# One turn of eight experts: the largest expert's overflow moves into four column strips and shares its turn with the smallest expert

## The chip, the cores and the metric

The kernel runs on one core of a Trainium2 chip. The metric is the time of one execution in microseconds (us). A core has TensorE (PE in the profile, its weight loads are PEld), VectorE (DVE), ScalarE (ACT), GpSimd (POOL) and SyncE (SP), which here issues the DMAs.

## The reference

Two layers over 256 latent tokens and 256 context tokens of width 1024. The last sub-layer of the second layer is a mixture of eight SwiGLU experts, two for each token. Only that part is touched by the change.

```python
N_EXPERTS = 8; TOP_K = 2; D_EXPERT = 3584; D_MODEL = 1024

def moe_swiglu(h, router_w, w1, w3, w2):
    logits = (h @ router_w).astype(jnp.float32)
    top_v, top_i = lax.top_k(logits, TOP_K)
    top_p = jax.nn.softmax(top_v, axis=-1)
    comb = jnp.sum(jax.nn.one_hot(top_i, N_EXPERTS, dtype=jnp.float32) * top_p[..., None], axis=-2).astype(h.dtype)
    y = jnp.zeros_like(h)
    for e in range(N_EXPERTS):
        y = y + comb[..., e:e + 1] * swiglu(h, w1[e], w3[e], w2[e])
    return y
```

Every tensor is float32. With the inputs that the reference draws (seed 0) its router sends 78, 61, 147, 94, 22, 46, 21 and 43 tokens to experts 0 to 7, worked out with the reference itself.

## The kernel before

**Experts, columns, turns.** Each expert gets only the tokens that chose it, gathered into slots. Expert 0 is column 0. The other seven are sorted by their token count on the chip: column 1 is the largest, column 2 the next, column 7 the third of them, and columns 3 to 6 the rest in falling order. `CAPS` gives the slots of each column. An expert with more tokens than slots gets its remaining tokens in an additional pass of a hardware loop at the end, `n_loop` of which always runs once for the last column.

The work is laid out in turns (`KINDS`, then one loop pass of kind S):

- **M**: one expert in 128 slots. Each weight unit is split by ACT (`w_hi`, L1355) and DVE (`w_lo`, L1713) into a high and a low part, and each product is three matmuls (`three`, L577 to L579) with 512 moving columns.
- **S**: one expert in 64 slots, no split. The weight unit in float32 is the moving operand, the 64 slots are the stationary operand in one half of the array's columns; the two halves (column strips of 64) work on different columns of the weights. Up part L1198, down part L1247.
- **P**: an M expert and an S expert at a time, each with its own weights.
- **B**: the largest expert alone, its first 128 slots as in M and 64 more as in S, from the same weight units.

Before, the turns are M, S, P, S, B, S and the loop pass S: seven turns for eight experts. `turn_m` and `turn_s` transpose the hidden values, `spread_of` turns a one-hot matrix, `scatter` puts the outputs back into token order in banks 6 and 7, and DVE adds them into an accumulator.

**Units and their ring.** An expert is 84 units of 512 KB: 56 for the up and gate matrices (7 column blocks `cb` of 8 units) and 28 for the down matrix. Units are loaded by SP in the order of `UNITS`. In P it is four units of the M expert, then four of the S expert, and so on. They land in a ring of 14 slots (`M_RING`). `moe_free` holds SP at L529 until the slot's former unit is done with: for kind "m" that is when DVE has split it (`lo_done`), for "s" and "b" when TensorE has used it (`s_used`). The split parts live in a second ring of 6 (`R`), and DVE and ACT split up to 5 units ahead (`LEAD`).

**Order on TensorE in a turn with both.** For each half `w` of each block: the M products of 4 units (24 matmuls), then the strips of 4 units, then, once a block, the transposes of the block before. In the down part: M products of 4 units, then the strips of 4 units. `gather_m` (L1051) and `gather_s` (L1062) collect the next turn's tokens in the third block of the down part. A matmul in float32 with both operands float32 (the strips) leaves two records in the trace, one with the split operands leaves one.

Of the kernel before, what the change touches and what calls it, by code (L numbers as in the profile page):

```python
# [152 lines left out]
def steps_of(kind):  # L153

    return {"M": [("m", 0), ("m", 1)], "S": [("s", 0), ("s", 1)],
            "B": [("m", 0), ("m", 1), ("s", 0), ("s", 1)], "P": [("m", 0), ("m", 1), ("s", 0), ("s", 1)]}[kind]
# [25 lines left out]
S_AT = {(tau, v): n for n, (tau, part, v) in enumerate(UNITS) if part != "m"}  # L182
# [40 lines left out]
def build(nc, x, c, ctx_in, c_ctx, w_ada, b_ada, norm_mix, norm_ffn, norm_out, w_in_even, gmlp_wt, gmlp_b,  # L223
# [3 lines left out]
    with es:  # L227
# [41 lines left out]
        cw_s = sb("cw_s", [P, LT])  # L269
        cslot_s = sb("cslot_s", [P, 1])  # L270
# [76 lines left out]
        sx_y, sx_sc, s_used = sem("sx_y"), sem("sx_sc"), sem("s_used")  # L347
        fin32, fin_tr, fin_out, stored = sem("fin32"), sem("fin_tr"), sem("fin_out"), sem("stored")
# [68 lines left out]
        def _(sp):  # L417
# [113 lines left out]
            def moe_free(n):  # L531

                if n < R:
                    u = max(u for u in range(U_MOE) if u % R == n)
                    sp.wait_ge(lo_done, u + 1)
                elif n < M_RING:
                    sp.wait_ge(h_done, 4 * KT)
                else:
                    tau, part, v = UNITS[n - M_RING]
                    if part == "m":  # L540
                        sp.wait_ge(lo_done, U_MOE + m_index(tau) * EXP_UNITS + v + 1)
                    else:
                        sp.wait_ge(s_used, s_index(tau) * EXP_UNITS + v + 1)
# [30 lines left out]
        def _(pe):  # L574
# [548 lines left out]

            def moe_turn(kind, tau, m, s, prev, adds, nxt):

                has_m, has_s, both = kind != "S", kind != "M", kind in ("B", "P")
# [8 lines left out]
                def old_outputs(v):  # L1135

                    if v in places:
                        x = places.index(v)
                        what, half = steps[x]
                        scatter(what, prev_m if what == "m" else prev_s, half, adds if x < 2 else adds + 1,  # L1140
                                prev_s if prev_kind in ("B", "P") and x == 0 else None)
# [17 lines left out]
                if has_m:  # L1159

                    pe.wait_ge(ga_lo, m + 1)
                if has_s:

                    pe.wait_ge(sx_g, tally(s, 1, 1))
                for cb in range(CB):
# [5 lines left out]
                    for w in range(2):  # L1171
# [19 lines left out]
                        if has_s:  # L1191
# [24 lines left out]
                    if cb == 3 and both:  # L1216

                        pe.wait_ge(sp_rdy, m + 1)
                        spread_of(onehot_s, cw_s).then_inc(sx_sp, 1)

                if prev_kind in ("M", "B", "P"):

                    pe.wait_ge(ey32, prev_m + 1)
                if prev_kind in ("S", "B", "P"):
# [7 lines left out]
                for cb in range(CB):  # L1232
# [9 lines left out]
                    if has_s:  # L1242
                        pe.wait_ge(sx_t, tally(s, CB, cb + 1))
                        for kt in range(4 * cb, 4 * cb + 4):
# [11 lines left out]
                    if cb == 2:  # L1256
# [3 lines left out]
                        if next_kind != "M":  # L1260
                            gather_s(next_s, 5 if next_kind in ("B", "P") else 0)
# [78 lines left out]
        def _(act):  # L1340
# [294 lines left out]
            def turned_s(s, cb, bank):  # L1635

                act.wait_ge(sx_mm, tally(s, CB, cb + 1))
                dst = hidden_s[:, cb * 4 * HALF:(cb + 1) * 4 * HALF].rearrange("p (j q c) -> p q j c", j=2, q=2)
                act.activation(dst, ps[:, bank, 0:256].rearrange("p (q j c) -> p q j c", q=2, j=2),
                               ACT.Copy).then_inc(sx_t, 1)  # L1640

            def moe_turn(kind, tau, m, s, prev, nxt):

                has_m, has_s, both = kind != "S", kind != "M", kind in ("B", "P")
                prev_kind, prev_m, prev_s = prev
                for v in range(EXP_UNITS):
                    if isinstance(tau, int):
                        split_to(min(splits_by(tau, v), U_MOE + len(M_ORDER)))
                    if v == 1 and prev_kind in ("M", "B", "P"):
                        out_hi(prev_m)  # L1650
                    if v % 8 == 0 and 8 <= v <= UP_UNITS:
# [5 lines left out]
                        if has_s:  # L1657
                            act.wait_ge(s_used, tally(s, EXP_UNITS, v))
                            gate = ps[:, 3 if both else 2 * (cb % 2), 0:256]
                            act.activation(ar(X_SS, 256), gate, ACT.Silu).then_inc(sx_silu, 1)  # L1660
                    if v % 8 == 4 and 12 <= v <= UP_UNITS + 4:
# [3 lines left out]
                        if has_s:  # L1665
                            turned_s(s, cb, (5, 3)[cb == CB - 1] if both else 6)
                    if v == UP_UNITS + 12:
# [3 lines left out]
                        if next_kind != "M":  # L1671
                            gathered_s(next_s, 5 if next_kind in ("B", "P") else 0)
# [26 lines left out]
        def _(dve):  # L1699
# [471 lines left out]
            def route_levels():  # L2171
# [5 lines left out]
                link(dve.memset(cap[:, 1:2], float(SLOTS + HALF)))  # L2177
# [49 lines left out]
            def one_hots_s(col, first):  # L2227
# [8 lines left out]
                dve.tensor_copy(cw_s[:, :].unsqueeze(2), src).then_inc(sx_oh, 1)  # L2236
# [12 lines left out]
            def out_scale_s(s, bank):  # L2249

                dve.wait_ge(s_used, tally(s, EXP_UNITS, EXP_UNITS))
                dve.wait_ge(sx_spr, tally(s, 1, 1))
                dve.tensor_scalar(ar(X_YS, BANK), ps[:, bank, :], cslot_s[:, 0:1], None, ALU.mult).then_inc(sx_y, 1)
# [22 lines left out]
            def moe_turn(kind, tau, m, s, prev, adds, nxt, m_col, s_col):  # L2276

                has_m, has_s, both = kind != "S", kind != "M", kind in ("B", "P")
# [3 lines left out]
                for v in range(EXP_UNITS):  # L2282
                    if isinstance(tau, int):
                        split_to(min(splits_by(tau, v), U_MOE + len(M_ORDER)))
                    if v == 0 and prev_kind in ("M", "B", "P"):
                        out_scale(prev_m)
                    if v == 0 and prev_kind in ("S", "B", "P"):
                        out_scale_s(prev_s, 4 if prev_kind == "S" else 7)
                    if v in (1, 2) and prev_kind in ("M", "B", "P"):
# [5 lines left out]
                    if v % 8 == 0 and 8 <= v <= UP_UNITS:  # L2295
# [5 lines left out]
                        if has_s:  # L2301
# [4 lines left out]
                            up = ps[:, 3, 256:512] if both else ps[:, 2 * (cb % 2) + 1, 0:256]  # L2306
                            dve.tensor_tensor(ar(X_HS, 256), up, ar(X_SS, 256), ALU.mult).then_inc(sx_hid, 1)  # L2307
# [6 lines left out]
                    if v == (33 if both else 25) and has_s:  # L2314
                        dve.wait_ge(sx_sp, tally(s, 1, 1))
                        dve.tensor_copy(ar(X_SPR, N_LAT), ps[:, 7, 0:256])
                        dve.tensor_copy(cslot_s[:, :], ps[:, 7, 256:257]).then_inc(sx_spr, 1)
# [10 lines left out]
                    if v == UP_UNITS + 5:  # L2328
                        if nxt != "S":
                            one_hots(m_col)  # L2330
                        if nxt != "M":
                            one_hots_s(s_col, SLOTS if nxt == "B" else 0)
# [64 lines left out]
```

## Time and profile before

| | |
|---|---|
| median of 3 runs | 2117.19 us (2114.79 to 2118.25) |
| the profiled execution | 2117.6 us, its span 2115.8 us |
| granted TensorE clock, mean | 0.945 |
| TensorE busy | 1896.9 us (90%) |
| VectorE, ScalarE busy | 916.8 us (43%), 729.6 us (34%) |
| DMA | 479.54 MB, mean 227 GB/s |

The table is of the profile's page. Shares of the whole span are a mean over stages that have different limits, so the rows to read are those of one turn at a time: how long it lasts, how busy TensorE is in it, and what the DMA engines move. A busy TensorE is not yet a full one, since ends of matmuls are modelled and overlap; the starts of successive groups are the better measure.

### The profile page before, as it was taken

To read this page: it belongs to the slowest core of one execution; us is meant where nothing else is said; L and a number is where in the kernel's file an instruction comes from. 1 tells how busy PE (TensorE), PEld (TensorE's weight loads), DVE (VectorE), ACT (ScalarE), POOL (GpSimd) and SP (SyncE) were. 2 spreads that over 40 slices of the span, in tenths; PEclk is the share of its full clock that TensorE was granted. 3 is DMA by queue.
4 is the path that set the end of the run, shared out by engine and by line. 5 is a ranking of instruction groups with operands and counts; after the bars stand their busy time and mean duration, and the time that the engine had idled before them with its cause. 6 is when DMAs were issued, how large, how long until landed. Compare 5 with 4: busy or idle time off the path is not lost.

```text
span 2115.8 us, 25988 instructions
## 1 busy us (share of the span) xinstructions
PE 1896.9 (90%) x10266; PEld 1346.8 (64%) x10266; DVE 916.8 (43%) x1290; ACT 729.6 (34%) x938; POOL 114.1 (5%) x122
## 2 busy tenths in 40 slices
PE   5999899999997788796659999999999999999987
PEld 2677577777785677676657874566654577664433
DVE  2432622332235656867647940355530366530002
ACT  3231221221223645555436730244420345410001
POOL 0000000000000122423300000000000000000000
PEclk8998999999998899898868999999999999999998
DMA  8634166343431322210136989999999965579994
GB/s 320 230 129 139 30 239 235 115 138 130 149 100 40 100 61 69 60 60 21 60 129 228 375 327 409 409 409 408 409 409 409 380 219 213 202 296 408 409 409 185
DMA packets 161692, 479.54 MB, mean 227 GB/s; under 512 B 14961, under 2 KB 58145, under 8 KB 155426
## 3 DMA queue, kind: packets, MB, share of 16 engines
q1 hardware_dynamic: 161570, 477.88, 60.4%
q8 instruction: 81, 1.33, 0.3%
q14 instruction: 41, 0.34, 0.0%
HBM read 476.77 MB, written 1.05 MB: 226 GB/s over the span
## 4 chain that ended last, share of the span: by engine, by line
PE 65%; DVE 12%; DMA 11%; SPq 4%; ACT 4%; issue 3%; POOL 1%; DVEq 0%; ACTq 0%
PE ps L577 13%; PE ps L579 13%; PE ps L578 13%; PE ps L1198 9%; PE ps L1247 4%; DMA arena<-in_moe_up 4%; SPq L529 4%; DMA arena<-in_moe_w 4%; DMA raw<-in_moe_up 3%; DVE w_lo L1713 3%; PE ps L591 2%; PE ps L610 2%; PE ps L1062 1%; ACT w_hi L1355 1%; DVE arena L1770 1%
## 5 line engine op out<-in xcount | busy, mean ns | idle before, releaser
L1713 DVE TENSOR_TENSOR w_lo<-raw,w_hi 128x1024 fp32r<-128x1024 f32 x242 | 302.7, 1258 | 455.2 <-ACT w_hi L1355 450.7
L1355 ACT ACTIVATE w_hi<-raw 128x1024 fp32r<-128x1024 f32 x242 | 254.0, 1056 | 463.3 <-PE ps L579 383.4
L577 PE MATMUL ps<-h_hi,w_hi 128*128 128x512 f32 (+1 forms) x736 | 292.8, 398 | 26.2 <-DVE h_lo L1757 22.8
L578 PE MATMUL ps<-h_hi,w_lo 128*128 128x512 f32 (+1 forms) x736 | 283.0, 385 | 0.0
L579 PE MATMUL ps<-h_lo,w_hi 128*128 128x512 f32 (+1 forms) x736 | 282.3, 384 | 0.0
L1713 DVE TENSOR_TENSOR w_lo<-arena,w_hi 128x1024 fp32r<-128x1024 f32 x144 | 173.6, 1222 | 91.7 <-ACT w_hi L1355 85.6
L577 PEld LDWEIGHTS ps<-h_hi,w_hi 128*128 128x128 f32 x736 | 147.5, 200 | 83.2 <-issue 53.7
L1198 PE MATMUL ps<-arena 128*64 128x256 f32 x1536 | 188.0, 385 | 13.3 <-DMA arena<-in_moe_up 7.1
L1355 ACT ACTIVATE w_hi<-arena 128x1024 fp32r<-128x1024 f32 x144 | 152.0, 1060 | 116.7 <-PE ps L579 46.8
L579 PEld LDWEIGHTS ps<-h_lo,w_hi 128*128 128x128 f32 x736 | 146.2, 199 | 26.2
L578 PEld LDWEIGHTS ps<-h_hi,w_lo 128*128 128x128 f32 x736 | 147.2, 200 | 23.8 <-issue 0.5
L1198 PEld LDWEIGHTS ps<-arena 128*64 128x64 f32 x1536 | 102.2, 136 | 87.9 <-DMA arena<-in_moe_up 28.0
L1198 PE MATMUL ps<-raw,arena 128*64 128x256 f32 x1152 | 137.8, 384 | 7.7 <-DMA raw<-in_moe_up 4.5
L577 PE MATMUL ps<-w_hi,s_hi 128*128 128x512 f32 x336 | 135.9, 404 | 4.3 <-DVE s_lo L2217 2.4
L579 PE MATMUL ps<-w_lo,s_hi 128*128 128x512 f32 x336 | 132.2, 393 | 0.0
L578 PE MATMUL ps<-w_hi,s_lo 128*128 128x512 f32 x336 | 132.1, 393 | 0.0
L577 PE MATMUL ps<-w_hi,h_hi 128*128 128x512 f32 (+1 forms) x328 | 118.2, 360 | 6.3 <-DVE arena L1914 6.3
L1198 PEld LDWEIGHTS ps<-raw,arena 128*64 128x64 f32 x1152 | 78.1, 137 | 62.6 <-DMA raw<-in_moe_up 18.8
L578 PE MATMUL ps<-w_hi,h_lo 128*128 128x512 f32 (+1 forms) x328 | 115.3, 351 | 0.0
L579 PE MATMUL ps<-w_lo,h_hi 128*128 128x512 f32 (+1 forms) x328 | 115.1, 351 | 0.0
L1247 PE MATMUL ps<-arena,scratch 128*64 128x512 f32 x384 | 97.4, 623 | 7.6 <-DMA arena<-in_moe_w 6.9
L2307 DVE TENSOR_TENSOR arena<-ps,arena 128x256 f32<-128x256 f32 x42 | 17.7, 422 | 194.8 <-ACT arena L1660 194.8
(345 smaller groups left out, 2507.7 us busy)
## 6 DMA issues: line engine op xcount, KB each, us to landing
arena<-in_moe_up SPq DMA_DIRECT2D x256, 512.0 KB, 9.9
raw<-in_moe_up SPq DMA_DIRECT2D x192, 512.0 KB, 9.4
arena<-in_moe_w SPq DMA_DIRECT2D x128, 512.0 KB, 12.8
raw<-in_moe_w SPq DMA_DIRECT2D x96, 512.0 KB, 14.2
raw<-in_ffn_w SPq DMA_DIRECT2D x66, 512.0 KB, 5.4
arena<-in_w_ada SPq DMA_DIRECT2D x32, 1024.0 KB, 5.4
raw<-in_w_in_odd SPq DMA_DIRECT2D x40, 512.0 KB, 3.5
scratch<-in_w_ada SPq DMA_DIRECT2D x16, 1024.0 KB, 5.7
```

Source lines behind the costliest of these rows:

```text
L529: sp.dma_start(moe_slot(n), src).then_inc(moe_in[n % M_RING], 16)
L577: pe.matmul(dst, s_h, m_h, start=start, stop=False, **kw)
L578: pe.matmul(dst, s_l, m_h, start=False, stop=False, **kw)
L579: return pe.matmul(dst, s_h, m_l, start=False, stop=stop, **kw)
L591: m = pe.matmul(ps[32 * j:32 * j + 32, bank, :], cond[:, a % KT, :], w[:, j * BANK:(j + 1) * BANK], start=start, stop=stop, skip_group_che ...
L610: pe.matmul(ps[:, 3, 0:width], ones, ar(NORM_AT[n] + kt % 2 * NT, width), start=(kt == 0), stop=(kt == KT - 1)).then_inc(sq_mm, 1)
L1062: i = pe.matmul(ps[:, bank, kt * HALF:(kt + 1) * HALF], part[:, t * D + kt * P:t * D + (kt + 1) * P], onehot_s[:, t, 0:HALF], start=(q == ...
L1198: i = pe.matmul(ps[64 * j:64 * j + 64, bank, at:at + 256], ar(X_G + kt * HALF, HALF), src[:, kk * BANK + 256 * j:kk * BANK + 256 * j + 256 ...
L1247: i = pe.matmul(ps[64 * j:64 * j + 64, 7 if both else 4, :], hidden_s[:, kt * HALF:(kt + 1) * HALF], src[:, j * BANK:(j + 1) * BANK], star ...
L1355: act.activation(w_hi[:, o % R, :], src, ACT.Copy).then_inc(hi_done, 1)
L1713: dve.tensor_tensor(w_lo[:, o % R, :], src, w_hi[:, o % R, :].bitcast(F32), ALU.subtract).then_inc(lo_done, 1)
L1770: m = dve.tensor_scalar(t[:, a:b], t[:, a:b], coef[:, kt, s:s + 1], adaT[:, layer, sh * KT + kt, s:s + 1], ALU.mult, ALU.add)
```

## The change

The turns become M, Q, S, P, S and the loop pass S: six turns for the same eight experts. The new kind Q runs column 1 (the largest) in 128 slots as in M with 32 more slots, and column 6 (the smallest) in 32 slots. Both groups of 32 slots are computed in column strips of 32, four at a time: strip `j` takes a quarter of the moving columns, 128 in the up part and 256 in the down part. The group `q = 0` reads the largest expert's units again (kind "b"), the group `q = 1` the smallest one's (kind "s"). A slot with a "b" unit comes free when `q = 0` has used it (`qx_used`). The caps become 128, 160, 128, 64, 64, 64, 32, 64. The largest expert's turn is now the second, right behind M, and kind B is gone. All units of all experts are loaded once, as before.

```diff
-KINDS = "MSPSBS"
-M_COL = {0: 0, 2: 2, 4: 1}
-S_COL = {1: 3, 2: 4, 3: 5, 4: 1, 5: 6, 6: 7}
-CAPS = [SLOTS, SLOTS + HALF, SLOTS, HALF, HALF, HALF, HALF, HALF]
+QUART = SLOTS // 4
+KINDS = "MQSPS"
+M_COL = {0: 0, 1: 1, 3: 2}
+S_COL = {1: 6, 2: 3, 3: 4, 4: 5, 5: 7}
+Q_TURN = KINDS.index("Q")
+S_BANK = {"S": 0, "P": 5, "Q": 7}
+CAPS = [SLOTS, SLOTS + QUART, SLOTS, HALF, HALF, HALF, QUART, HALF]
...
-            for part in {"M": "m", "S": "s", "B": "b", "P": "ms"}[kind]:
+            for part in {"M": "m", "S": "s", "Q": "bs", "P": "ms"}[kind]:
...
                     if part == "m":
                         sp.wait_ge(lo_done, U_MOE + m_index(tau) * EXP_UNITS + v + 1)
+                    elif part == "b":
+                        sp.wait_ge(qx_used, v + 1)
                     else:
...
+                if kind == "s" and n == s_index(Q_TURN):
+                    for k in range(4):
+                        dst = ps[:, 6 + k // 2, k % 2 * 256:k % 2 * 256 + 256]
+                        j = (4 * half + k) // 2 * QUART
+                        for q in range(2):
+                            at = X_YS + q * 256 + k % 2 * P
+                            i = pe.matmul(dst, arena[j:j + QUART, at:at + P],
+                                          arena[j:j + QUART, X_SPR + q * N_LAT:X_SPR + (q + 1) * N_LAT],
+                                          start=(q == 0), stop=(q == 1), tile_position=(j, 0))
+                    i.then_inc(sx_sc, 1)
+                    return
...
+            def spread_strips(q):
+
+                for t in range(LT):
+                    hot = onehot_s[:, t, q * QUART:(q + 1) * QUART].bitcast(F32)
+                    for j in range(4):
+                        pe.matmul(ps[j * QUART:(j + 1) * QUART, 7, t * P:(t + 1) * P], hot, ident, start=True, stop=True,
+                                  skip_group_check=True)
...
+                        if quart:
+                            for q in range(2):
+                                for k in range(4):
+                                    src = s_unit(v + k) if q else x_unit(v + k)
+                                    for kk in range(2):
+                                        kt = 2 * k + kk
+                                        rows = ar(X_G + kt * HALF + q * QUART, QUART)
+                                        for j in range(4):
+                                            at = 256 * q + P * w
+                                            i = pe.matmul(ps[j * QUART:(j + 1) * QUART, 3, at:at + P], rows,
+                                                          src[:, kk * BANK + P * j:kk * BANK + P * (j + 1)],
+                                                          start=(kt == 0), stop=(kt == KT - 1), skip_group_check=True)
+                                    i.then_inc(s_used if q else qx_used, 1)
+                        elif has_s:
...
+                            if both and cb == 1 and prev_kind in ("M", "Q", "P"):
+
+                                pe.wait_ge(ey32, prev_m + 1)
...
+                        if quart:
+                            spread_strips(0).then_inc(qx_sp, 1)
+                        else:
+                            spread_of(onehot_s, cw_s).then_inc(sx_sp, 1)
+                    if cb == 4 and quart:
+
+                        pe.wait_ge(qx_spr, 1)
+                        spread_strips(1).then_inc(sx_sp, 1)
...
+                    if quart:
+                        for q in range(2):
+                            for kt in range(4 * cb, 4 * cb + 4):
+                                src = s_unit(UP_UNITS + kt) if q else x_unit(UP_UNITS + kt)
+                                rows = hidden_s[:, kt * HALF + q * QUART:kt * HALF + (q + 1) * QUART]
+                                for j in range(4):
+
+                                    i = pe.matmul(ps[j * QUART:(j + 1) * QUART, 7, 256 * q:256 * q + 256], rows,
+                                                  src[:, 256 * j:256 * j + 256], start=(kt == 0 and q == 0),
+                                                  stop=(kt == EXP_KT - 1), skip_group_check=True)
+                                i.then_inc(s_used if q else qx_used, 1)
```

ACT and DVE follow with the same number of instructions in a block: the gate, the product and the turned copy address the strips' values in the new order, DVE scales the two halves of the output one by one, and copies the spread matrix in two parts (at units 33 and 41). `one_hots_q` makes the two one-hot matrices.

## Rows read from the trace of the kernel before

**Rows 1.** The page: the span in 40 slices of 52.9 us each.

```profile
PE   5999899999997788796659999999999999999987
...
PEclk8998999999998899898868999999999999999998
DMA  8634166343431322210136989999999965579994
GB/s 320 230 129 139 30 239 235 115 138 130 149 100 40 100 61 69 60 60 21 60 129 228 375 327 409 409 409 408 409 409 409 380 219 213 202 296 408 409 409 185
```

**Rows 2.** Busy time by stretches: turns S, P, S, B, the last two.

```profile
core 0: us, PE busy (x) PEld busy (x) DVE busy (x) ACT busy (x) POOL busy (x), PEclk, DMA share, GB/s
1247.60:1347.50 99.90, 95.26 (x661) 49.79 (x660) 12.96 (x24) 11.33 (x21) 0.00 (x0) 0.97 1.00 396
1347.50:1565.30 217.80, 209.53 (x1168) 144.31 (x1168) 113.76 (x114) 95.04 (x112) 0.00 (x0) 0.99 1.03 409
1565.30:1672.20 106.90, 98.14 (x679) 50.58 (x675) 13.63 (x25) 9.12 (x18) 0.00 (x0) 1.00 1.03 409
1672.20:1879.60 207.40, 207.40 (x1166) 143.31 (x1168) 117.73 (x115) 100.91 (x113) 0.00 (x0) 1.00 0.63 225
1879.60:2090.00 210.40, 192.49 (x1277) 91.32 (x1274) 18.27 (x35) 11.96 (x30) 0.00 (x0) 0.99 0.99 394
```

**Rows 3.** Waits of SP's queue inside turn B (1680 to 1895 us): total, times, longest.

```profile
SPq L529 <- PE ps L1198: 112.1, 63, 8.1
SPq L529 <- PE ps L1247: 54.5, 26, 9.8
```

**Rows 4.** Timeline of TensorE in turn B without the M products: start, length, what.

```profile
1758.96 1.95 PE L1198 MATMUL ps<-raw,arena 128*64 128x256 f32 x16
1760.73 1.90 PE L1198 MATMUL ps<-arena 128*64 128x256 f32 x16
1762.56 0.66 PE L1076 MATMUL ps<-con,arena 128*128 128x128 f32 x4
1763.05 0.38 PE L1088 MATMUL ps<-con,arena 128*128 128x128 f32 x2
1768.85 3.67 PE L1198 MATMUL ps<-arena 128*64 128x256 f32 x32
1778.12 1.95 PE L1198 MATMUL ps<-arena 128*64 128x256 f32 x16
...
1797.28 3.67 PE L1198 MATMUL ps<-arena 128*64 128x256 f32 x32
```

**Rows 5.** Timeline of TensorE, down part of turn B: its strips.

```profile
1866.87 3.65 PE L1247 MATMUL ps<-arena,scratch 128*64 128x512 f32 x16
1876.12 3.65 PE L1247 MATMUL ps<-arena,scratch 128*64 128x512 f32 x16
```

**Rows 6.** Timeline of weight loads at 30 us: strips of 32 columns, 512 moving.

```profile
30.01 0.13 PEld L591 LDWEIGHTS ps<-arena,cond 128*32 128x32 f32 x4 [0.30 <-issue]
30.44 0.13 PEld L591 LDWEIGHTS ps<-arena,cond 128*32 128x32 f32 x4 [0.30 <-issue]
30.87 0.13 PEld L591 LDWEIGHTS ps<-arena,cond 128*32 128x32 f32 x4 [0.30 <-issue]
```

**Rows 7.** Timeline of TensorE before turn B: both gathers (L1051, start of L1062).

```profile
1649.01 2.00 PE L1051 MATMUL ps<-onehot,s_hi 128*128 128x128 f32 x16
1650.85 1.95 PE L1051 MATMUL ps<-onehot,s_lo 128*128 128x128 f32 x16
1652.64 0.35 PE L1062 MATMUL ps<-onehot_s,s_hi 128*128 128x64 f32 x2
1652.83 0.39 PE L1062 MATMUL ps<-onehot_s,s_lo 128*128 128x64 f32 x2
1653.05 0.39 PE L1062 MATMUL ps<-onehot_s,s_hi 128*128 128x64 f32 x2
```

**Rows 8.** Busy time by stretches, columns as in rows 2: right behind turn M.

```profile
1248.00:1249.00 1.00, 1.00 (x14) 0.64 (x11) 0.98 (x1) 0.00 (x0) 0.00 (x0) 1.00 0.00 0
```

**Rows 9.** DMA issues in turn B: count, KB each, median us from issue to landing.

```profile
arena<-in_moe_up SPq DMA_DIRECT2D x22, 512.0 KB, 5.3
raw<-in_moe_up SPq DMA_DIRECT2D x16, 512.0 KB, 4.9
```

**Rows 10.** Waits of TensorE in turn P (1360 to 1575 us).

```profile
PE ps L1198 <- DVE arena L2307: 6.5, 6, 1.4
```

**Rows 11.** The down strips over the span: durations, first and last start.

```profile
L1247 PE MATMUL ps<-arena,scratch x384: 592/592/1116, 1315.7 to 2087.8; 128*64 128x512 f32 x192
L1247 PE MATMUL ps<-raw,scratch x288: 592/592/1061, 1308.1 to 2078.4; 128*64 128x512 f32 x144
```

**Rows 12.** The up strips over the span: count, durations, first and last start.

```profile
L1198 PE MATMUL ps<-arena x1536: 379/379/431, 1252.8 to 2050.9; 128*64 128x256 f32 x192
L1198 PE MATMUL ps<-raw,arena x1152: 379/379/431, 1247.6 to 2040.2; 128*64 128x256 f32 x192
```

More of the change, by code:

```diff
@@ L155, in steps_of @@
     return {"M": [("m", 0), ("m", 1)], "S": [("s", 0), ("s", 1)],
-            "B": [("m", 0), ("m", 1), ("s", 0), ("s", 1)], "P": [("m", 0), ("m", 1), ("s", 0), ("s", 1)]}[kind]
+            "Q": [("m", 0), ("m", 1), ("s", 0), ("s", 1)], "P": [("m", 0), ("m", 1), ("s", 0), ("s", 1)]}[kind]
 def adds_before(tau):
@@ L181 @@
 M_AT = {(tau, v): n for n, (tau, part, v) in enumerate(UNITS) if part != "s"}
-S_AT = {(tau, v): n for n, (tau, part, v) in enumerate(UNITS) if part != "m"}
+S_AT = {(tau, v): n for n, (tau, part, v) in enumerate(UNITS) if part == "s"}
 M_ORDER = [M_AT[tau, v] for tau in range(FIXED) if KINDS[tau] != "S" for v in range(EXP_UNITS)]
@@ L347, in build @@
         sx_y, sx_sc, s_used = sem("sx_y"), sem("sx_sc"), sem("s_used")
+        qx_used, qx_sp, qx_spr = sem("qx_used"), sem("qx_sp"), sem("qx_spr")
         fin32, fin_tr, fin_out, stored = sem("fin32"), sem("fin_tr"), sem("fin_out"), sem("stored")
@@ L1122, in spread_of @@
                 return i
+            def spread_strips(q):
[4 more added lines that the diff above has]
+                                  skip_group_check=True)
+                for t in range(LT):
+                    hot = onehot_s[:, t, q * QUART:(q + 1) * QUART].bitcast(F32)
+                    for j in range(4):
+                        i = pe.matmul(ps[j * QUART:(j + 1) * QUART, 7, 256:257], hot, cw_s[:, q * LT + t:q * LT + t + 1],
+                                      start=(t == 0), stop=(t == LT - 1), skip_group_check=True)
+                return i
             def moe_turn(kind, tau, m, s, prev, adds, nxt):
-                has_m, has_s, both = kind != "S", kind != "M", kind in ("B", "P")
+                has_m, has_s, both, quart = kind != "S", kind != "M", kind in ("Q", "P"), kind == "Q"
                 prev_kind, prev_m, prev_s = prev
@@ L1140, in old_outputs @@
                         scatter(what, prev_m if what == "m" else prev_s, half, adds if x < 2 else adds + 1,
-                                prev_s if prev_kind in ("B", "P") and x == 0 else None)
+                                prev_s if prev_kind in ("Q", "P") and x == 0 else None)
                 def m_unit(v):
@@ L1633, in turned_hi, with turned_s @@
                 act.activation(h_hi[:, cb * BANK:(cb + 1) * BANK], ps[:, 6, :], ACT.Copy).then_inc(et_hi, 1)
-            def turned_s(s, cb, bank):
+            def turned_s(s, cb, bank, quart):
                 act.wait_ge(sx_mm, tally(s, CB, cb + 1))
-                dst = hidden_s[:, cb * 4 * HALF:(cb + 1) * 4 * HALF].rearrange("p (j q c) -> p q j c", j=2, q=2)
-                act.activation(dst, ps[:, bank, 0:256].rearrange("p (q j c) -> p q j c", q=2, j=2),
-                               ACT.Copy).then_inc(sx_t, 1)
+                dst = hidden_s[:, cb * 4 * HALF:(cb + 1) * 4 * HALF]
+                if quart:
+                    dst = dst.rearrange("p (j q c) -> p q j c", j=4, q=2)
+                    out_of = ps[:, bank, 0:256].rearrange("p (q j c) -> p q j c", q=2, j=4)
+                else:
+                    dst = dst.rearrange("p (j q c) -> p q j c", j=2, q=2)
+                    out_of = ps[:, bank, 0:256].rearrange("p (q j c) -> p q j c", q=2, j=2)
+                act.activation(dst, out_of, ACT.Copy).then_inc(sx_t, 1)
             def moe_turn(kind, tau, m, s, prev, nxt):
-                has_m, has_s, both = kind != "S", kind != "M", kind in ("B", "P")
+                has_m, has_s, both, quart = kind != "S", kind != "M", kind in ("Q", "P"), kind == "Q"
                 prev_kind, prev_m, prev_s = prev
@@ L1648, in moe_turn @@
                         split_to(min(splits_by(tau, v), U_MOE + len(M_ORDER)))
-                    if v == 1 and prev_kind in ("M", "B", "P"):
+                    if v == 1 and prev_kind in ("M", "Q", "P"):
                         out_hi(prev_m)
@@ L1658, in moe_turn @@
                             act.wait_ge(s_used, tally(s, EXP_UNITS, v))
-                            gate = ps[:, 3 if both else 2 * (cb % 2), 0:256]
-                            act.activation(ar(X_SS, 256), gate, ACT.Silu).then_inc(sx_silu, 1)
+                            if quart:
+                                act.wait_ge(qx_used, v)
+                                gate = ps[:, 3, :].rearrange("p (q w c) -> p q w c", q=2, w=2)[:, :, 0]
+                                act.activation(ar(X_SS, 256).rearrange("p (q c) -> p q c", q=2), gate,
+                                               ACT.Silu).then_inc(sx_silu, 1)
+                            else:
+                                gate = ps[:, 3 if both else 2 * (cb % 2), 0:256]
+                                act.activation(ar(X_SS, 256), gate, ACT.Silu).then_inc(sx_silu, 1)
                     if v % 8 == 4 and 12 <= v <= UP_UNITS + 4:
@@ L2235, in one_hots_s, with one_hots_q @@
                 src = comb[:, :, bass.ds(col, 1)] if not isinstance(col, int) else comb[:, :, col:col + 1]
-                dve.tensor_copy(cw_s[:, :].unsqueeze(2), src).then_inc(sx_oh, 1)
+                dve.tensor_copy(cw_s[:, 0:LT].unsqueeze(2), src).then_inc(sx_oh, 1)
+            def one_hots_q(m_col, s_col):
+                for q, (col, first) in enumerate(((m_col, SLOTS), (s_col, 0))):
+                    for t in range(LT):
+                        dve.tensor_scalar(onehot_s[:, t, q * QUART:(q + 1) * QUART], iota[:, 0:QUART], float(first),
+                                          rank[:, t, col:col + 1], ALU.add, ALU.is_equal)
+                    i = dve.tensor_copy(cw_s[:, q * LT:(q + 1) * LT].unsqueeze(2), comb[:, :, col:col + 1])
+                i.then_inc(sx_oh, 1)
             one_hots(0)
@@ L2252, in out_scale_s @@
                 dve.wait_ge(sx_spr, tally(s, 1, 1))
+                if s == s_index(Q_TURN):
+                    dve.wait_ge(qx_used, EXP_UNITS)
+                    dve.tensor_scalar(ar(X_YS, 256), ps[:, bank, 0:256], cslot_s[:, 0:1], None, ALU.mult)
+                    dve.tensor_scalar(ar(X_YS + 256, 256), ps[:, bank, 256:512], cslot_s[:, 1:2], None,
+                                      ALU.mult).then_inc(sx_y, 1)
+                    return
                 dve.tensor_scalar(ar(X_YS, BANK), ps[:, bank, :], cslot_s[:, 0:1], None, ALU.mult).then_inc(sx_y, 1)
@@ L2276, in moe_turn @@
             def moe_turn(kind, tau, m, s, prev, adds, nxt, m_col, s_col):
-                has_m, has_s, both = kind != "S", kind != "M", kind in ("B", "P")
+                has_m, has_s, both, quart = kind != "S", kind != "M", kind in ("Q", "P"), kind == "Q"
                 prev_kind, prev_m, prev_s = prev
@@ L2313, in moe_turn @@
                         dve.tensor_copy(cslot[:, :], ps[:, 7, 256:257]).then_inc(sp_rdy, 1)
-                    if v == (33 if both else 25) and has_s:
+                    if v == 33 and quart:
+                        dve.wait_ge(qx_sp, 1)
+                        dve.tensor_copy(ar(X_SPR, N_LAT), ps[:, 7, 0:256])
+                        dve.tensor_copy(cslot_s[:, 0:1], ps[:, 7, 256:257]).then_inc(qx_spr, 1)
+                    if v == (41 if quart else 33 if both else 25) and has_s:
+                        at = N_LAT if quart else 0
                         dve.wait_ge(sx_sp, tally(s, 1, 1))
-                        dve.tensor_copy(ar(X_SPR, N_LAT), ps[:, 7, 0:256])
-                        dve.tensor_copy(cslot_s[:, :], ps[:, 7, 256:257]).then_inc(sx_spr, 1)
+                        dve.tensor_copy(ar(X_SPR + at, N_LAT), ps[:, 7, 0:256])
+                        dve.tensor_copy(cslot_s[:, quart:quart + 1], ps[:, 7, 256:257]).then_inc(sx_spr, 1)
                     if tau == 0 and v == 10:
```

46 lines of the change are left out of this document (29 added, 17 removed).

## The prediction

> **What bounds the kernel now.** I read the slices of the page first [rows 1]. About 410 GB/s is the most that the DMA engines hold anywhere in the expert part, and from slice 25 on they stand at it, except in slices 32 to 36, where they fall as low as 202 GB/s with TensorE at 9 tenths. The stretches by turn say the same in microseconds [rows 2]. S and P move 396 to 409 GB/s: they last as long as their weights take. P and the S behind it, 252 units in 217.8 + 106.9 = 324.7 us, give 1.289 us for a unit. Turn B lasts 207.4 us with TensorE busy in all of it, at 225 GB/s for 84 units. There SP waits at L529 for the strips 89 times, 166.6 us in all [rows 3]: the ring is full and TensorE empties it. So B is bound by TensorE, S and P by the DMA. The time that the DMA engines lose in B is (1 - 225/409) x 207.4 = 93 us.
>
> **What the change does to the sum.** The bytes stay the same. Turn B (84 units) and one S turn (84 units) become one turn Q of 168 units, whose DMA time is 168 x 1.289 = 216.5 us. The question is whether TensorE does Q in that time. Q's work on TensorE is that of B, with these differences.
>
> *The split products* (24 matmuls for 4 units, up and down) are the same. *The up strips.* In B, 32 records of 256 columns take 3.60 us (1758.96 to 1762.56), 16 pairs of strips [rows 4]. In Q the same half block is 128 records of 128 columns, 32 sets of four strips. That four strips run side by side is shown early in the trace: sets of four loads of 32 columns, each in front of four 512-column records, start 0.43 us apart [rows 6], which is what a pair of 512-column records takes in the down strips (3.65 us for 8 pairs, some 0.43 each) [rows 5]. So four strips cost what two do, a 128-column set is a quarter of that, 0.107 us, and 32 sets are 3.4 us. The lower end is this 0.107. For the upper end the trace has nothing that shows TensorE being fed faster for long: a pair of load and matmul comes every 0.11 us, in the gathers (0.22 for two) [rows 7] and in B's strips (3.60 / 32) [rows 4]. Four such pairs would make a set 0.43 us. The set needs one pair every 0.027 us. I take 0.111, the floor of the array with a little on it, because in each of those rows the pace is explained by the array or by the 128-column load, and because four loads of 32 columns take 0.13 us together [rows 6] and lie under matmuls. 14 half blocks x (32 x 0.111 - 3.46, B's 16 pairs of 0.216) = +1.3 us.
>
> *The down strips*: 64 records of 256 columns for four units of each, 16 sets of 0.21 us = 3.4 us against 3.65 [rows 5]: nothing. *Spread matrix*: two times 16 small matmuls in strips for one `spread_of`, +1 us. *Scatter* inside Q is now M's, 16 records of the split kind against 16 of the float32 kind, -1 to -2 us. The added waits (`ey32`, `qx_spr`, ACT's `qx_used`) are on things done several us earlier; behind them on TensorE stands the next block, on ACT the splits; 0, up to 1 us each once. Sum for TensorE: 207.4 + 1.3 + 1 - 1.5 = 208 us, under the 216.5 of the weights.
>
> **The ring in Q.** A "b" slot is held until `q = 0` has used it. At the end of M the ring is full and the DMA engines stand still (0 GB/s) [rows 8]. Q then frees nothing during its first M products. These take 9.27 us less the strips' 3.60, so 5.7 (1768.85 to 1778.12) [rows 4], and the first use by `q = 0` ends some 0.6 later. From an issue to its landing on empty queues it is 4.9 to 5.3 us [rows 9]. So unit 15 lands 5.7 + 0.6 + 5.1 = 11.4 us into Q, and the last, unit 168, 153 x 1.289 = 197 us later, at 209. TensorE then needs some 2 us more: Q lasts 211 us. After that start it doesn't stop the DMA: a group of 8 units takes 10.3 us to land, TensorE takes 19.16 / 2 = 9.6 for it (1778.12 to 1797.28) [rows 4], and a freed slot's next unit is due 7 to 9 us after its release, against 5 from issue to landing.
>
> *M in front of Q* has to gather for a split expert too: `gather_m`, 3.6 us (1649.01 to 1652.64) [rows 7]. Before, that ran in an S turn, beside the DMA. M is bound by TensorE at its end (ring full) [rows 8], so +3.6 us on the path. *Q's outputs* are scattered in the S turn behind it, with 16 records for each half of the strips' part, some 2 us more each; S has 106.9 - 98.1 = 9 us idle there [rows 2]: hidden. If that cover were gone, +4.
>
> **The sum.** From the end of M to the last down strips, before: 2088.4 - 1247.6 = 840.8 us (the last starts at 2087.8) [rows 11]. After: 3.6 + 211 (Q) + 420 units of S, P, S, S x 1.289 = 541.3, + 2 at the end = 757.9. Less by 83. The DMA's side gives: 93 us lost in B no longer, 3 us of the first S (396 for 409 GB/s) [rows 2] neither, 3.6 and 6 lost at the start of Q: -86. I take -85. The profiled execution took 2117.6 us, 1.8 over its span and 0.4 over the median: 2117.6 - 85 = 2032.6, by the median 2032.
>
> **Rivals.** *A: four strips are not fed fast enough.* Q issues 128 pairs in a burst of 3.5 us where nothing so far asks for more than one in 0.11 us for long. For it: no row shows it. Against: sets of four start together [rows 6]. Q's group has 10.3 - 9.6 = 0.7 us to spare, so it starts to cost at 0.13 us a set, and then 14 x 32 = 448 sets pay the rest. At 0.25 us: 448 x 0.12 = +54, 2086. At 0.20: +31, 2063. Chance 0.17 for a set of 0.14 to 0.30 us. *B: the same to the end, slower than before.* At four separate pairs, 0.43 us a set, Q grows by 448 x 0.30 = 134 us: 2166. It decides from 0.13 + 85 / 448 = 0.32 us a set. Chance 0.08. *C: the ring.* If a "b" slot's later release keeps the DMA waiting 1 to 2 us in each of Q's 21 groups, or DVE's chain holds the strips as in P (6.5 us in 6 waits) [rows 10] without cover, it is +20 to +40: 2052 to 2072. Chance 0.10. *D: it doesn't do what it says.* If an expert overflows its slots, the loop takes another turn of 84 x 1.289 = 108 us: 2140. Before, the strips have 2688 up records [rows 12], 448 for each of six turns, so nobody overflowed. The counts are 147 for 160 slots, 21 for 32, and 61 and 46 for 64. Chance 0.01.
>
> On A and B a rule bears. The Trainium skill, "TensorE: Matmul & The Clock Gate", in "Wait — 56ns, not 53.3ns?", says that matmuls never start less than about 25 ns apart however small, and that without the hardware decoder the sequencer spends about 62 ns on each, which then binds. Within a set the trace's loads start closer than 25 ns (four in 0.13 us with their length) [rows 6], but that is a burst, and no row here shows the pace over many sets. By 25 ns a set would be 0.10 us, under the array's time, and my forecast would stand; by 62 ns it would be 0.25 us, an estimate from that page, and the time would be the 2086 of rival A.
>
> **How the numbers follow.** The forecast, 2032, has 0.62 with 2020 to 2047 as its own range: without the start of Q (-6) and `gather_m` (-4) at the low end, with some late units in Q at the high end. A is 0.17, C 0.10, B 0.08, D 0.01, and 0.02 for a loss that happens to eat the gain. The range goes from 2018 to 2088, which takes in C and most of A and leaves out B and D. About 0.2% is what a measurement of this kernel can tell from no change. Faster by more: 0.62 + 0.17 + 0.10 = 0.89; same 0.02; slower 0.09.
>
> **What would show it.** Right: six turns; Q of 205 to 217 us with over 390 GB/s behind its first 15 us, groups of 10.3 us and strips of 3.5 to 3.7 us for `q` 0 and 1 together; S, P, S, S as before at 409 GB/s; no slice at 200 GB/s. Wrong in the cost of strips: the same strips last 6 us or more and the DMA falls below 380 GB/s while TensorE has no idle. Wrong in the ring: strips short, but SP waits for them with TensorE idle. An up strip beyond six turns' worth would show rival D.

## The result and the profile after

| | before | after |
|---|---|---|
| median, us | 2117.34 (2114.79 to 2118.25, 4 runs) | 2061.95 (2056.94 to 2066.64, 4 runs) |
| profiled execution | 2117.6, span 2115.8 | 2066.64, span 2064.8 |
| granted TensorE clock, mean | 0.945 | 0.934 |
| ratio | | 0.974, 95% interval 0.9715 to 0.9765 |

The change takes 55 us off (2.6%). The forecast was 2032 in a range of 2018 to 2088: the direction and the range hold. The narrower range of 2020 to 2047, which the forecast gave to its own mechanism, does not, and 30 of the 85 us are missing. The slices of the page of the changed kernel, which answer to [rows 1]:

```profile
PE   5899899999998977887757999889999999998987
...
PEclk8998999999998988998886999999999999999998
DMA  8633166334531222221105987889999999999993
GB/s 327 236 132 133 41 216 241 133 96 150 180 96 61 72 82 62 62 62 42 62 1 187 339 316 285 332 337 367 407 409 409 406 408 409 409 408 409 409 408 154
```

The hole at 202 to 219 GB/s late in the span is gone. In its place slices 25 to 28 (1239 to 1445 us) hold 285 to 367 GB/s: short of 409, and for long. Busy time by stretches, columns as in [rows 2], of the changed kernel: turn Q, the S turn behind it, and P, S, S:

```profile
1254.00:1494.80 240.80, 218.78 (x2909) 177.37 (x2907) 114.19 (x117) 95.12 (x113) 0.00 (x0) 0.94 0.91 346
1494.80:1600.50 105.70, 98.80 (x678) 53.28 (x676) 12.39 (x24) 6.98 (x16) 0.00 (x0) 0.97 1.03 409
1600.50:2035.70 435.20, 405.27 (x2458) 234.54 (x2454) 133.65 (x150) 109.91 (x145) 0.00 (x0) 1.00 1.01 403
```

Behind Q it is as forecast: 105.7 + 435.2 = 540.9 us for 420 units, against 541.3. (The cut between the second and the third stretch lies some 4 us before the end of that S turn's down strips; the sum doesn't depend on it.) The missing time is in Q: 240.8 us, not 211. It moves 346 GB/s, and TensorE has 22 us of idle time in it. So Q is bound by neither: something makes the two wait for each other. The waits of TensorE in Q (1255 to 1475 us: total, times, longest), the answer to [rows 10]:

```profile
PE ps L1239 <- DVE arena L2410: 21.6, 6, 4.1
PE ps L1127 <- DVE arena L2371: 0.4, 1, 0.4
```

L1239 is the new up strips, L2410 is DVE's product of gate and up for the strips of the block before. Bank 3 holds both, so the first strips of a block may not start before that product has been taken. Six waits, one in each block but the first. What a block looks like, on TensorE without the split products (start, length, what, idle before and its releaser):

```profile
1309.07 1.90 PE L1239 MATMUL ps<-raw,arena 128*32 128x128 f32 x32 [3.73 <-DVE arena L2410]
1310.72 3.72 PE L1239 MATMUL ps<-arena 128*32 128x128 f32 x96
1314.36 0.66 PE L1085 MATMUL ps<-con,arena 128*128 128x128 f32 x4
1314.86 0.38 PE L1097 MATMUL ps<-con,arena 128*128 128x128 f32 x2
1320.64 1.08 PE L1239 MATMUL ps<-arena 128*32 128x128 f32 x32
1321.54 2.80 PE L1239 MATMUL ps<-raw,arena 128*32 128x128 f32 x96
1324.28 0.44 PE L1138 MATMUL ps<-con,onehot 128*128 128x128 f32 x2
...
1334.11 6.49 PE L1239 MATMUL ps<-arena 128*32 128x128 f32 x128 [3.49 <-DVE arena L2410]
```

The second strips of a block last 3.64 us (1320.64 to 1324.28), as forecast. The first wait 3.73 us and then last 5.29 us (1309.07 to 1314.36), at a mean granted clock of 0.68. The next block's first strips start 25.0 us later (1334.11). Why DVE is late stands in its own timeline over the same stretch, and in ACT's:

```profile
1296.66 2.48 DVE L1798 TENSOR_TENSOR w_lo<-arena,w_hi 128x1024 fp32r<-128x1024 f32 x2
1305.59 2.48 DVE L1798 TENSOR_TENSOR w_lo<-arena,w_hi 128x1024 fp32r<-128x1024 f32 x2 [6.45 <-ACT w_hi L1429]
1308.00 0.68 DVE L2402 TENSOR_TENSOR arena<-ps,arena 128x512 f32<-128x512 f32 x1
1308.60 0.41 DVE L2410 TENSOR_TENSOR arena<-ps,arena 128x256 f32<-128x256 f32 x1
...
1304.50 1.06 ACT L1429 ACTIVATE w_hi<-arena 128x1024 fp32r<-128x1024 f32 x1 [6.62 <-DMA arena<-in_moe_up]
1305.76 1.06 ACT L1429 ACTIVATE w_hi<-arena 128x1024 fp32r<-128x1024 f32 x1 [0.20 <-DMA arena<-in_moe_up]
```

DVE is idle for 6.45 us, then splits two units (L1798), and only then forms the products L2402 and L2410. ACT waits as long for a unit to land. These two units are `b4` and `b5`, the second half block's, split ahead of time. The program puts them ahead of the product. The chain of work shows where the landing comes from:

```profile
1298.37 7.38 DMA arena<-in_moe_up
1305.76 1.07 ACT w_hi L1429
1306.85 0.52 DVE w_lo L1798
1307.38 0.62 issue
1308.00 0.68 DVE arena L2402
1308.68 0.34 DVE arena L2410
...
1309.07 2.94 PE ps L1239 x50
```

SP could issue that unit only at 1298.37, because it goes into the slot of a "b" unit that the strips of the half block before (1295.98 to 1299.6) had just used. So it is a circle: strips, free slot, landing, split, product, strips. It has a length of its own, some 25 us a block, where the transfer needs 20.6 (16 units of 1.289). The wait can be added up from it. TensorE was ready for the strips at 1305.34, and from the landing (1305.76) to the strips (1309.07) the chain takes 3.3 us. So the unit would have had to land 3.7 us after its issue, and took 7.4.

### The profile page after: what moved, and what is told of

The parts are those of the page before. It is cut to its first block, busy times and chain, and to the rows that moved or that the text cites. A ratio compares the mean times of both kernels' runs of the same rounds, so it can differ in the third digit from the quotient of the medians.

```text
span 2064.8 us, 28192 instructions
## 1 busy us (share of the span) xinstructions
PE 1825.0 (88%) x11392; PEld 1339.3 (65%) x11392; DVE 908.8 (44%) x1282; ACT 719.2 (35%) x923; POOL 113.9 (6%) x122
## 4 chain that ended last, share of the span: by engine, by line
PE 62%; DMA 14%; DVE 13%; ACT 4%; issue 3%; SPq 3%; POOL 1%; DVEq 0%; ACTq 0%
PE ps L586 13%; PE ps L587 12%; PE ps L588 12%; DMA arena<-in_moe_up 7%; PE ps L1250 4%; DMA raw<-in_moe_up 3%; DVE w_lo L1798 3%; DMA arena<-in_moe_w 3%; PE ps L1321 3%; SPq L536 2%; PE ps L600 2%; PE ps L1239 2%; PE ps L619 2%; ACT w_hi L1429 1%; PE ps L1071 1%
## 5 line engine op out<-in xcount | busy, mean ns | idle before, releaser
L1798 DVE TENSOR_TENSOR w_lo<-raw,w_hi 128x1024 fp32r<-128x1024 f32 x242 | 302.7, 1258 | 468.9 <-ACT w_hi L1429 466.2
L1798 DVE TENSOR_TENSOR w_lo<-arena,w_hi 128x1024 fp32r<-128x1024 f32 x144 | 173.3, 1222 | 135.0 <-ACT w_hi L1429 131.2
L1250 PE MATMUL ps<-arena 128*64 128x256 f32 x1024 | 128.6, 387 | 14.4 <-DMA arena<-in_moe_up 8.4
L1250 PEld LDWEIGHTS ps<-arena 128*64 128x64 f32 x1024 | 66.8, 136 | 68.8 <-DMA arena<-in_moe_up 28.6
L1250 PE MATMUL ps<-raw,arena 128*64 128x256 f32 x768 | 93.2, 385 | 8.7 <-DMA raw<-in_moe_up 5.0
L586 PE MATMUL ps<-s_hi,w_hi 128*128 128x512 f32 (+1 forms) x240 | 89.9, 374 | 6.0 <-DVE s_lo L2145 6.0
L587 PE MATMUL ps<-s_hi,w_lo 128*128 128x512 f32 (+1 forms) x240 | 88.4, 368 | 0.0
L588 PE MATMUL ps<-s_lo,w_hi 128*128 128x512 f32 (+1 forms) x240 | 88.3, 368 | 0.0
```

The costliest lines, as they stand in the source:

```text
L586: pe.matmul(dst, s_h, m_h, start=start, stop=False, **kw)
L587: pe.matmul(dst, s_l, m_h, start=False, stop=False, **kw)
L588: return pe.matmul(dst, s_h, m_l, start=False, stop=stop, **kw)
L1250: i = pe.matmul(ps[64 * j:64 * j + 64, bank, at:at + 256], ar(X_G + kt * HALF, HALF), src[:, kk * BANK + 256 * j:kk * BANK + 256 * j + 256 ...
L1798: dve.tensor_tensor(w_lo[:, o % R, :], src, w_hi[:, o % R, :].bitcast(F32), ALU.subtract).then_inc(lo_done, 1)
```

## Experiments

Theory 1: the product waits in DVE's (and the gate in ACT's) program order behind two splits whose units land late. Theory 2: the ring itself starves the DMA queue, whatever the order. Theory 3: four strips cost more than forecast. Each time is a median of 4 runs, and its ratio is to the kernel before, measured beside it.

**The product ahead of the splits.** On ACT and on DVE alike, in turn Q only:

```diff
-                    if isinstance(tau, int):
+                    if isinstance(tau, int) and not (quart and v <= UP_UNITS and (v % 8 == 7 or v and v % 8 == 0)):
                         split_to(min(splits_by(tau, v), U_MOE + len(M_ORDER)))
...
+                    if isinstance(tau, int) and quart and v <= UP_UNITS and v and v % 8 == 0:
+                        split_to(min(splits_by(tau, v), U_MOE + len(M_ORDER)))
```

The second piece stands behind the products of that step.

> In turn Q, ACT's gate and DVE's product of the block just finished now go ahead of the splits of the next two units (those of units 8cb+4 and 8cb+5), on both engines; nothing else changes. Theory 1 (order on DVE): the six waits of the strips for DVE's product, 3.5 to 4.5 us each, and the half clock behind them come from these two splits waiting for units that land late. Then the waits go, the first strips of each block take 3.6 us, Q falls from 241 to 214 to 220 us and the time to 2032 to 2042 us. Theory 2 (the ring itself): the late release of the largest expert's slots starves the DMA queue whatever DVE does; then the wait only moves to the next split products, Q stays at 235 to 241 us and the time at 2056 to 2062 us.

Measured: 2034.75 us (2029.66 to 2042.36), ratio 0.9624 (0.9591 to 0.9657). Turn Q by the same view as above:

```profile
1247.10:1463.10 216.00, 210.53 (x2909) 167.80 (x2907) 114.90 (x117) 95.70 (x113) 0.00 (x0) 0.99 0.98 386
```

Q has gone from 240.8 to 216.0 us and from 346 to 386 GB/s, and no wait for the product is left in it. Of TensorE's waits that are left, the largest is for the late units themselves:

```profile
PE ps L586 <- DVE w_lo L1800: 4.4, 5, 1.7
```

Theory 1 holds, theory 2 falls: with the same late release of the slots the DMA is kept busy. The clock in Q is 0.99, not 0.94. The gate and the product changed places with two splits, and by the medians 27 us came back.

**Fewer units ahead.** The dose: with a lead of 4 one late unit stands ahead of the product, with a lead of 3 none.

```diff
     if KINDS[tau] != "S":
-        ahead = v + LEAD + 1 if (KINDS + "S")[tau + 1] != "S" else min(v + LEAD + 1, EXP_UNITS)
+        lead = LEAD - 1 if KINDS[tau] == "Q" and 0 < v < EXP_UNITS - LEAD else LEAD
+        ahead = v + lead + 1 if (KINDS + "S")[tau + 1] != "S" else min(v + lead + 1, EXP_UNITS)
```

(and `LEAD - 2` in the second run)

> In turn Q the splits run 4 units ahead in place of 5, so only one late unit (8cb+4), not two, stands ahead of DVE's product. Theory 1: each of the six waits gets shorter by one unit's landing, 1.3 us, and the strips spend less at half clock: 8 to 15 us less, 2047 to 2054 us. Theory 2: no change, 2058 to 2065 us. If a lead of 5 is needed for the split products, they wait and it gets slower, over 2066 us.

> In turn Q the splits run 3 units ahead in place of 5, so no unit of the next group of eight stands ahead of DVE's product, by the same edit as the lead of 4. By theory 1 the waits for the product go as they did when it was put ahead of the splits: 2033 to 2040 us, after 2062 for a lead of 5 and 2050 for 4. If a short lead makes the split products wait at each group, more than 2045 us.

Measured: 2049.87 us (2048.50 to 2052.26) with 4, 2034.94 us (2029.85 to 2036.21) with 3. So 2062, 2050, 2035 for two, one and no late unit in front of the product. The waits of TensorE fall along: 21.6 us with 5 (above), then with 4

```profile
PE ps L1240 <- DVE arena L2411: 16.2, 6, 4.2
```

and none with 3. Both ends were as theory 1 had them. A lead of 3 costs the split products little: they wait for DVE 4.7 us in 5 times, inside the time that the transfer needs anyway. It is the simplest mend, and ties with the one above.

**The slots free early.** The order in `UNITS` says "ms" for Q in place of "bs", and both groups of strips read the smallest expert's units, so TensorE does the same work. Left out is the proper result for the largest expert's tokens beyond 128.

```diff
-            for part in {"M": "m", "S": "s", "Q": "bs", "P": "ms"}[kind]:
+            for part in {"M": "m", "S": "s", "Q": "ms", "P": "ms"}[kind]:
...
-                                    src = s_unit(v + k) if q else x_unit(v + k)
+                                    src = s_unit(v + k)
...
-                                src = s_unit(UP_UNITS + kt) if q else x_unit(UP_UNITS + kt)
+                                src = s_unit(UP_UNITS + kt)
```

> The strips of the largest expert's 32 further slots read the smallest expert's units (so this part of the output is not the reference's: the tokens of the largest expert beyond 128 get wrong values), and the largest expert's slots come free at the split, as in turn P. TensorE's work is the same to the instruction. Theories 1 and 2 both: the units land in time, Q is bound by the DMA, 214 to 220 us, time 2032 to 2042 us. Theory 3 (four strips cost more than forecast, by feeding or by the clock they leave): Q stays above 230 us, time above 2052 us.

Measured: 2033.32 us (2027.33 to 2037.19). Q lasts 214.0 us at 392 GB/s; the six waits are 7.0 us in all, with 1.8 the longest, as in turn P before [rows 10]. This cuts the circle at its other joint, the release, and gives the same by the medians, 29 us. So the late release is a cause too, but only together with the order: either one alone costs nothing that these times can tell. The units here take 8.4 to 8.9 us from issue to landing, longer than the 7.4 above, and it does no harm. So a slow landing is not the cause by itself either. Theory 3 falls: the strips are the same, and Q runs at the rate of its weights.

**The clock by itself.** 16 matmuls whose result nobody reads fill TensorE's wait, in five of the six blocks:

```diff
+                        if quart and cb >= 2 and w == 0:
+                            for f in range(16):
+                                pe.matmul(ps[:, 4, :], s_hi[:, 2048 + f % 8 * P:2048 + (f % 8 + 1) * P],
+                                          s_hi[:, 2048:2048 + BANK], start=True, stop=True)
                         if both and cb >= 1 and w == 0:
 
                             pe.wait_ge(sx_hid, s * CB + cb)
```

> The changed kernel with 16 more matmuls (of kinds and sizes like the split products, 0.23 us each, 3.6 us in all, result unused) on TensorE in turn Q right in front of the first strips of blocks 2 to 6, where it would wait 3.5 to 4.5 us for DVE's product. Nothing is taken off the chain that it waits for. If the strips behind the waits (5.1 to 6.2 us in place of 3.4) are long only because TensorE's clock fell in the idle time, they take 3.4 us now, the slots come free that much earlier, and the time falls by 5 to 12 us, to 2050 to 2057 us. If they are long for a reason of their own (feeding, weights not landed), they stay over 5 us and the time stays or grows, 2060 to 2070 us.

Measured: 2054.26 us (2052.69 to 2064.53), beside 2061.46 (2054.14 to 2063.04) for the changed kernel measured again next to it: within what was expected, but the spreads overlap, so the times alone don't settle it. For the length of the strips the records do:

```profile
1321.37 3.79 PE L1229 MATMUL ps<-s_hi 128*128 128x512 f32 x16
1326.30 3.70 PE L1243 MATMUL ps<-arena 128*32 128x128 f32 x128 [1.14 <-DVE arena L2414]
```

With the array kept at work, the first strips of a block take 3.70 us by their records. In the changed kernel, behind waits of 2.8 to 4.1 us, they took 5.0 to 6.5. What that is worth in time is less sure. The up strips of Q with the filler, then those of the changed kernel measured next to it (the last figures are the first and the last start):

```profile
L1243 PE MATMUL ps<-arena x1024: 272/273/418, 1255.8 to 1411.6; 128*32 128x128 f32 x171
L1239 PE MATMUL ps<-arena x1024: 272/273/423, 1256.7 to 1419.2; 128*32 128x128 f32 x171
```

From first to last it is 155.8 us, not 162.5, so 6.7 us less in this pair of executions, and 7 us by the medians. That is an estimate of what the fallen clock costs in these five blocks, out of the 27 us. The wait doesn't go with the clock: in the block shown the filler and what is left of the wait take 3.79 + 1.14 us, where the same block of the changed kernel waited 3.49.

**Turn P too, and Q in the fourth place.** The first edit with `both` for `quart`; then that with

```diff
-KINDS = "MQSPS"
-M_COL = {0: 0, 1: 1, 3: 2}
-S_COL = {1: 6, 2: 3, 3: 4, 4: 5, 5: 7}
-S_BANK = {"S": 0, "P": 5, "Q": 7}
+KINDS = "MPSQS"
+M_COL = {0: 0, 1: 2, 3: 1}
+S_COL = {1: 3, 2: 4, 3: 6, 4: 5, 5: 7}
+S_BANK = {"S": 0, "P": 7, "Q": 7}
```

> As the run with the product ahead of the splits in Q (2034.75 us), now in turn P too. P has the same waits (6.5 us in 6) but is bound by its weights' transfer: its waits go, its length stays 216 to 218 us, and the time is the same, 2030 to 2038 us. If these waits cost P something after all, 2026 to 2031 us.

> The same with the turn order M P S Q S S. P frees its M slots at the split and so has no start-up loss behind M, while Q starts behind a turn bound by the DMA. If the start of Q behind a full ring costs the 6 us that were forecast, this is 4 to 7 us faster than the order M Q S P S S: 2026 to 2031 us. If not, the same, 2031 to 2038 us.

Measured: 2037.62 us (2029.11 to 2038.10) and 2030.46 us (2026.61 to 2032.85). In P the waits had lain under the transfer, and taking them away changes nothing that can be told (ratio 0.9619 beside 0.9624). The order with Q fourth gave the best median of all, ratio 0.9597 (0.9580 to 0.9614), against 0.9619 (0.9595 to 0.9643) with Q second: the intervals overlap, so 7 us is what the medians say and no more. Q itself is not shorter in the fourth place: 219.2 us at 400 GB/s, against 216.0 at 386 in the second place with the product first:

```profile
1566.20:1785.40 219.20, 212.85 (x2908) 169.59 (x2906) 115.40 (x116) 96.73 (x112) 0.00 (x0) 0.98 1.01 400
```

The order alone, in the changed kernel:

> Turn order M P S Q S S in place of M Q S P S S, everything else the same (the gather for P and for Q goes to bank 7). Theories 1 and 2: what Q loses is in Q, six waits wherever it stands, time 2058 to 2066 us. If a part of the loss is that Q starts behind M with a full ring and a fallen clock, Q gets shorter behind an S turn and P, with its early release, takes that start better: 2045 to 2055 us.

> The changed kernel as it is, on the same chip as the three above and as a control for the order M P S Q S S, which took 2056 us on another: 2057 to 2067 us.

Measured: 2056.09 us (2052.42 to 2058.42), and 2061.46 for the changed kernel again. The first lies between the two ranges that were expected of it, so it decides for neither. By ratio to before it is 0.9716 (0.9693 to 0.9739) against 0.9737 (0.9713 to 0.9760): not told apart. What Q loses goes with it to its new place, 22.3 us in 6 waits:

```profile
PE ps L1239 <- DVE arena L2410: 22.3, 6, 5.6
```

## Why the prediction was right, and where it was not

**What bounds what.** Right. In turn B, bound by TensorE, the DMA engines lost 93 us. Merging its leftover with another expert took 55 us off the time, and S, P, S, S ran at their old rate (540.9 us for a forecast of 541.3).

**The strips.** Right, and rivals A and B are out. The forecast had 0.111 us for a set of four, 3.55 us for 128 records; 3.64 us with the switch to the next work was measured, where B's 32 records took 3.60 [rows 4]. The strips add nothing to Q: four times the instructions ride in the same time. A pair of load and matmul came every 28 ns over a whole burst (3.64 us / 128). Of the rule that was weighed, in the Trainium skill's "TensorE: Matmul & The Clock Gate", under "Wait — 56ns, not 53.3ns?", the sequencer's 62 ns for each matmul did not bind here, and the floor of about 25 ns between two starts holds for this mean but not within a set. There four start inside 0.03 us (length, busy time and records of TensorE and of its weight loads, clock, DMA share, GB/s):

```profile
1320.64:1320.67 0.03, 0.03 (x4) 0.03 (x4) 1.00 0.99 410
```

**`gather_m` in turn M.** Right in kind. Q starts at 1254.0, 6.4 us later than the S turn did (1247.6), for a forecast of 3.6. In the runs with the product first and with a lead of 4, and in the changed kernel measured again, M took some 3.2 us more than before: that is the term. The other 3.2 are a clock that fell in the gathers of this execution (below).

**The ring in Q.** This is the step that failed, with 30 us: Q was 240.8 and not 211. It said that a freed slot's next unit is due 7 to 9 us after its release, against 5 from issue to landing. Both numbers were off. The 5 was taken from turn B, where the DMA engines had time to spare (225 GB/s) [rows 9]; here the unit on the chain took 7.4. And the unit was called due when the split products want it. But DVE and ACT split unit `b5`, in program order, before they form the product that the strips of the first half block wait for. So it was due 3.7 us after its issue (above), and even 5 us from issue to landing would have been too long. The sign that the prediction named for this came too, strips short and SP waiting for them with TensorE idle (1255 to 1475 us, as in [rows 3]):

```profile
SPq L536 <- PE ps L1239: 110.5, 36, 11.3
```

The row was there: in P the same wait cost 6.5 us in 6 [rows 10], with slots that come free at the split. I used it as a rival (C: "or DVE's chain holds the strips as in P", 2052 to 2072 us, chance 0.10) and did not ask what the later release would make of it. That rival is what happened, at 2062. So the wide range holds because it had room for this rival and for A, and not because the ring was reckoned rightly.

**The start of Q.** Forecast as 6 us lost to a full ring. With the circle gone, Q takes 216.0 and 214.0 us (product first, slots free early), against 211 reckoned, and the time comes to 2034.75 and 2033.32 for a forecast of 2032. So the sum was sound for a kernel without the circle. How much of it is the start was not measured by itself: moving Q away from there gave 7 us by the medians, inside their spread. In the two profiled executions it is 5.4 us from the end of M to the last down strips, and half of that lies in the last two S turns, which no edit touched.

**No overflow.** Right: the strips' up records are 1792 of 64 columns, four turns of 448, and 1792 of 32 columns, one turn: no further pass ran.

## What to carry to other kernels

Where engines run far ahead of each other, ask of each prefetch step what stands behind it in its engine's program order: work for the future that has to wait for a transfer must not stand ahead of work that somebody needs now. Here a buffer that is held longer cost nothing by itself and neither did the order; the two together closed a circle of 25 us where the transfer needed 20.6. A stage with idle time on its busiest engine (here 22 of 240.8 us) and a DMA rate under its best (346 of 409 GB/s) is worth searching for such a circle. Here the program order was a cheap place to cut it.

## What the runs showed of the hardware

TensorE's clock also fell where nothing idled by the records. In the changed kernel's turn M the two gathers stand back to back, 64 matmuls of 128 and 64 moving columns, each behind a load of 128 columns. Stretches of that execution (length, TensorE busy, granted clock, DMA share, GB/s):

```profile
1224.00:1226.00 2.00, 2.00 (x21) 1.00 0.97 373
1226.00:1228.00 2.00, 2.00 (x17) 0.81 1.02 416
1228.00:1230.00 2.00, 2.00 (x11) 0.50 0.88 361
1230.00:1232.00 2.00, 2.00 (x9) 0.50 0.01 4
```

Some 5 us into the gathers (from 1222.1) the clock went from 2.4 to 1.2 GHz with the engine busy by its records, and a pair of gather matmuls took 0.43 us, not 0.22. The same happened in the run with the slots free early. The other eight profiled executions with both gathers in M, the changed kernel measured again among them, kept the full clock over theirs. That is some 3 us on the path in some executions and none in others, and may be one source of the 0.5% spread between runs of one kernel here. What made it fall in two and not in the others was not tried.

Behind the strips' waits in Q the granted clock fell in all six blocks of both profiled executions of the changed kernel, where the waits were 2.8 to 4.3 us. It stayed full behind the six waits of the run with the slots free early, 0.5 to 1.8 us, and behind one of 2.9 us in the run with Q fourth.

Four column strips of 32 run side by side with their weight loads, one set of four records with 128 float32 columns each every 0.107 us, sustained over 32 sets (the changed kernel, 3.3 us between the first and the last set). In three of the ten profiled executions with a turn Q, one strip burst of its 14 is longer than the rest at full clock: by 1.0 us with the product first, where the trace shows a gap of 0.64 us and names "issue", by 1.2 us with the product first in P too, and by 0.3 us with a lead of 3. What it is was not tried.
